# Softmax factors of the first attention on ScalarE, and eight modulation tiles moved behind the attention's row maxima

## The reference

```
mod = silu(c) @ w_mod + b_mod            # 6 chunks of 1024 per layer, for x and for ctx
h   = rms_norm(x) * (1 + scale) + shift  # scale, shift: chunks of mod
qkv = h @ w_qkv                          # 16 query heads, 4 key and value heads, head size 64
q, k = rope(q), rope(k)                  # latent tokens
s   = q @ k.T                            # blocks of 128 queries: up to 3 near key blocks and the 256 context keys
m   = max(max(s), sink)
e   = exp(s - m)
p   = e / (sum(e) + exp(sink - m))
o   = p @ v ;  y = o @ w_o               # y is then gated by another chunk of mod
```

## Time and profile before

| what | value |
|---|---|
| median of the runs | 2658.0 us |
| the profiled execution | 2659.49 us, its span 2656.7 us |
| mean granted TensorE clock over the span | 0.965 of full speed |
| TensorE matmuls busy | 2461.1 us (93%) |
| TensorE weight loads busy | 2036.7 us (77%) |
| VectorE busy | 1693.7 us (64%) |
| ScalarE busy | 1088.6 us (41%) |
| GpSimd busy | 94.3 us (4%) |
| stretch of the attention loop | 205.9 to 405.3 us of the span |

### The profile page before, as it was taken

How to read it: one execution, slowest core, us unless ns; L and a number is a source line. 1 busy time by engine, 2 the same in 40 slices (tenths; PEclk the granted TensorE clock), 3 DMA queues, 4 the chain that set the end, 5 groups by cost and what they waited for, 6 DMA issues and landing times. The chain is left out here.

```text
span 2656.7 us, 32750 instructions
## 1 busy us (share of the span) xinstructions
PE 2461.1 (93%) x12252; PEld 2036.7 (77%) x12252; DVE 1693.7 (64%) x2746; ACT 1088.6 (41%) x1739; POOL 94.3 (4%) x111
## 2 busy tenths in 40 slices
PE   6968899899999999899998899998989999999999
PEld 5865558699999997687777688886766666777777
DVE  6666778765646466655553634445347997569986
ACT  4424443431313133423333422333446663377764
POOL 0000000000000000000000000000000330020000
PEclk8989999899999999889999999998999999999999
DMA  6220004133323232011111122222121221149995
GB/s 255 84 91 0 1 1 159 51 133 127 127 96 127 103 127 82 22 48 48 40 40 48 63 97 96 101 91 94 64 72 44 72 71 64 49 164 341 338 336 183
DMA packets 78131, 275.62 MB, mean 104 GB/s; under 512 B 8800, under 2 KB 9312, under 8 KB 77856
## 3 DMA queue, kind: packets, MB, share of 16 engines
q1 hardware_dynamic: 74016, 265.74, 28.5%
q10 hardware_dynamic: 3968, 7.88, 0.9%
HBM read 271.49 MB, written 2.10 MB: 103 GB/s over the span
## 5 line engine op out<-in xcount | busy, mean ns | idle before, releaser
L645 PE MATMUL DP<-HH,WL 128*128 128x384 f32 (+2 forms) x1408 | 517.7, 368 | 28.3 <-DVE WL L638 22.5
L646 PE MATMUL DP<-HH,WH 128*128 128x384 f32 (+2 forms) x1408 | 504.6, 358 | 0.0
L647 PE MATMUL DP<-HL,WH 128*128 128x384 f32 (+2 forms) x1408 | 504.5, 358 | 0.0
L638 DVE TENSOR_TENSOR WL<-RAW,WH 128x1024 fp32r<-128x1024 f32 x230 | 280.8, 1223 | 218.7 <-ACT WH L611 212.0
L645 PE MATMUL DP<-A,WL 128*128 128x384 f32 (+2 forms) x1072 | 381.7, 356 | 22.6 <-issue 8.4
L646 PE MATMUL DP<-A,WH 128*128 128x384 f32 (+2 forms) x1072 | 379.1, 354 | 0.0
L647 PE MATMUL DP<-A,WH 128*128 128x384 f32 (+2 forms) x1072 | 378.8, 353 | 0.0
L611 ACT ACTIVATE WH<-RAW 128x1024 fp32r<-128x1024 f32 x230 | 241.2, 1050 | 292.6 <-PE DP L647 205.0
L645 PEld LDWEIGHTS DP<-HH,WL 128*128 128x128 f32 x1408 | 267.5, 190 | 66.8 <-DVE WL L638 31.8
L646 PEld LDWEIGHTS DP<-HH,WH 128*128 128x128 f32 x1408 | 267.6, 190 | 29.2 <-issue 5.2
L647 PEld LDWEIGHTS DP<-HL,WH 128*128 128x128 f32 x1408 | 267.3, 190 | 25.5
(11 more groups left out here) (419 smaller groups left out, 3863.7 us busy)
## 6 DMA issues: line engine op xcount, KB each, us to landing
RAW<-in_stream SPq DMA_DIRECT2D x326, 512.0 KB, 3.3
MRAW<-in_stream SPq DMA_DIRECT2D x168, 512.0 KB, 5.4
MATS<-in_ssm ACTq DMA_DIRECT2D x16, 256.0 KB, 2.6
X<-in_x SPq DMA_DIRECT2D x8, 384.0 KB, 10.0
BW<-in_rel ACTq DMA_DIRECT2D x4, 512.0 KB, 3.5
out<-X SPq DMA_DIRECT2D x8, 256.0 KB, 2.0
COND<-in_cond SPq DMA_DIRECT2D x1, 1024.0 KB, 4.9
CONST<-in_const SPq DMA_DIRECT2D x1, 256.0 KB, 4.9
```

Source lines behind the costliest of these rows:

```text
L638: dve.tensor_tensor(WL[:, w, :], RAW[:, nxt.u % RING, :], WH[:, w, :].bitcast(F32), ALU.subtract).then_inc(raw_done[nxt.u % RING], 1)
L645: pe.matmul(out, al, bh, start=first, stop=False)
L646: pe.matmul(out, ah, bh, start=False, stop=False)
L647: return pe.matmul(out, ah, bl, start=False, stop=last)
```

## The change

- `rides_after` gives one modulation tile for r = 2 to 5 and none for r = 6 to 9. The other eight (20 to 27) go into the stream behind the last qkv tile and ahead of the first `attn_w_o` tile, and VectorE takes one at the end of its program for each odd block n below 16 of the attention, behind `maxima(n+2)`.
- `mod_add_bias` for the twelve tiles moves behind the attention loop.
- The denominators' transpose, reciprocal and transpose back leave VectorE. ScalarE makes the factors of block n-1 as exp(-ln(d)) on all 64x512 values, in `denominators(n-1)`: a Ln from PSUM and an Exp in place, put into its program of block n between `sink_term(n+1)` and the second exponentials.
- `normalise` on VectorE waits for that and keeps its two multiplications.

```diff
 def rides_after(t):
-    return (1 if t < 4 else 2) if t < 8 else 0
+    return 1 if t < 4 else 0
+
+def rides_within(n):
+    return 1 if n % 2 and n < 16 else 0
...
     for t in (8, 9, 0, 1, 2, 3, 4, 5, 6, 7, 10, 11):
         dense("attn_w_qkv", t * P)
         for _ in range(rides_after(t)):
+            mod(0, next(rides))
+    for n in range(24):
+        for _ in range(rides_within(n)):
             mod(0, next(rides))
     dense("attn_w_o", 0)
...
+            def denominators(n):
+                act.wait_ge(sem("attended"), values_through(n))
+                if n:
+                    act.wait_ge(sem("normalised"), 2 * n)
+                over = RC[0:64, :, :, :].rearrange("p e j n -> p (e j n)")
+                act.activation(over, XP[64:P, 2 + n % 2, :], ACT.Ln).then_inc(sem("denominators"), 1)
+                act.wait_ge(sem("denominators"), 2 * n + 1)
+                act.activation(over, over, ACT.Exp, scale=-1.0).then_inc(sem("denominators"), 1)
...
                     exps(first + i)
                     if i == 0 and n + 1 < len(WORK):
                         sink_term(n + 1)
+                    if i == 0 and n:
+                        denominators(n - 1)
...
+            denominators(n)
             mixed_high(n, g, b)
...
             rope_low(9)
-            mod_add_bias(dve, 12, lambda n, o=0: slice(o + 16, o + 16 + n))
...
             def normalise(n):
-                dve.wait_ge(sem("attended"), values_through(n))
                 bank_of = 2 + n % 2
-                turned = RCT[:, :].rearrange("p (b n) -> p b n", n=32)
-                dve.transpose(RCT[:, :], XP[64:P, bank_of, :]).then_inc(sem("denominators"), 1)
-                dve.wait_ge(sem("denominators"), 3 * n + 1)
-                dve.reciprocal(RCS[:, :], turned[:, :, 0:1].rearrange("p b n -> p (b n)")).then_inc(sem("denominators"), 1)
-                dve.wait_ge(sem("denominators"), 3 * n + 2)
-                dve.transpose(RC[0:64, :, :, :].rearrange("p e j n -> p (e j n)").rearrange("p (b n) -> p b n", n=32),
-                              RCS[:, :].unsqueeze(2).to_broadcast((64, 16, 32))).then_inc(sem("denominators"), 1)
-                dve.wait_ge(sem("denominators"), 3 * n + 3)
+                dve.wait_ge(sem("denominators"), 2 * n + 2)
...
                 if n + 2 < len(WORK):
                     maxima(*WORK[n + 2][0:4])
+                mods(rides_within(n))
+            mod_add_bias(dve, 12, lambda n, o=0: slice(o + 16, o + 16 + n))
             normalise(n)
```

More of the change, by code:

```diff
@@ L259, in backbone_kernel @@
             RC = sb(s0, "RC", [P, 2, 2, P])
-            RCT = sb(s0, "RCT", [64, 512])
-            RCS = sb(s0, "RCS", [64, 16])
             OU = sb(s0, "OU", [P, 2, 2, P])
```

## The result

| | before | changed |
|---|---|---|
| median of the runs | 2658.7 us (11 runs, 2656.5 to 2666.2) | 2667.3 us (11 runs, 2662.3 to 2672.2) |
| changed against before | | 1.0029, 95% interval 1.0019 to 1.0039 |
| profiled execution, its span | 2659.5, 2656.7 us | 2663.9, 2662.2 us |
| VectorE, ScalarE busy | 1693.7, 1088.6 us | 1653.1, 1119.0 us |

The change made the kernel slower, by about 0.3%. The forecast was 2660, and the range, 2649 to 2669, holds the median. The case with the highest chance (0.55: no difference that a measurement tells from none) was not the one that came.

What follows compares the result with a forecast made beforehand. VectorE was taken to bound the late projection and mostly TensorE the attention; -14.7 us in the projection and +16.6 us in the attention gave +1.9 us on a 2658.0 median, put down as 2660, range 2649 to 2669.

Steps and rivals of the forecast that it cites:

- The projection: Late projection steps: without eight modulation tiles TensorE becomes the bound and value groups start at 160.3 instead of 175.06, -14.7 us.
- the tail: End of the projection: last swap at 152.2, then RoPE, high parts, low parts and split, value groups at 160.3.
- the value groups' clock: Value groups after the projection: starting at full clock would give 2.6 us more; not counted, 0.87 assumed before and after.
- No table reload: Ln and Exp pair in the attention: no activation table loads; the rival with reloads cost +61 us, chance 0.02.
- the attention's term: Attention loop: the pair delays exponentials 1 by 1.17 us and moved tiles delay some blocks, +16.6 us in sum.
- the four-key blocks: Seven attention blocks: key block 3 already waits for exponentials 1, so all 1.17 us reach TensorE, +8.2 us.
- The five-key blocks: Eight attention blocks: key block 3 has 0.2 to 0.5 us of slack, so 0.6 late each, +4.8 us.
- The four two-key blocks: Blocks 5, 11, 17, 20, no tile ahead: ScalarE's chain to `rows_low` replaces VectorE's, 0.1 us each, +0.4 us.
- the rival's 2668: Attention loop: grown stalls make the clock fall, 1.75 us each time; 2665 with three falls, 2677 with ten; chance 0.20.
- The three two-key blocks behind a tile: Blocks 2, 8, 14: a 2.71 us tile replaces 1.77 us on VectorE, +0.95 on `rows_low` each, +2.9 us.
- the other five tiles: Moved tiles ahead of four-key blocks: VectorE ends 3.6 us behind the sink term, `rows_high` 3.9, so covered at no cost.
- The margin within a projection step: Late projection: swap to split done takes 7.2 us, ending 8.3 us into TensorE's 9.2 us step.

Runs made afterwards that it cites:

- e3: The eight tiles moved, factors left on VectorE, and the tiles' sums left out, against the kernel before: 2642.7 us, ratio 0.9931 to 0.9956.
- e9: The change itself run again on another chip, against the kernel before: 2666.5 us, ratio 1.0024 to 1.0048, loop 220.6 us.
- e2: Only the factors moved to ScalarE, all twelve tiles left in the projection, against the kernel before: 2678.1 us, ratio 1.0070 to 1.0100.
- e1: Only the eight tiles moved, factors left on VectorE, against the kernel before: 2670.4 us, ratio 1.0043 to 1.0069.
- e4: The change with ScalarE's pair behind exponentials and queries, VectorE reordered and tiles at other blocks, against the kernel before: 2636.4 us, ratio 0.9910 to 0.9935.

## Why the prediction was right in its range and too low in its sum

**The projection** went as argued: TensorE's step of 9.2 us became the bound (9.18), the tail is that of the forecast (8.13 us from swap to value groups, 8.1 forecast), the value groups start at 159.4 (160.3 forecast), 14.7 us were forecast and 14.0 (e3) to 14.8 (traces) measured. Not counting the value groups' clock was right too: 0.87 before and after, behind a gap of 6.21 us.

**No table reload, loads free, bias additions free**: the last activation table load up to 490 us is still the one asked for by name at the start, as in the earlier trace rows, e3's loop is that of before, and from the last sum to the norm it is 75.3 us in both kernels. The Trainium skill, "ScalarE: Activation LUTs", section "Table sets: the hidden batching unit", would have charged the pair with loads if another set had been active; the trace agrees in that it has no load beside the pair.

**The step that failed is the attention's term**, +16.6 us, where the loop measured +24.2. The mechanism was right: the pair is in a hand-over from ScalarE to TensorE that had no slack, and every four-key block pays its whole length. The size was wrong in two ways.

- The clean cost was 20.9 us, 4.3 over the forecast. I let the chain overlap at each end by 0.1 us, as exponentials 1 did behind the sink term. Here the Ln starts 0.03 after the sink term's end, and exponentials 1 start 0.03 after the Exp's: neither overlaps, so the hand-over is 1.41 and not 1.17. In the four-key blocks, 1.43 for 1.17, that makes 1.8 us over the seven. The five-key blocks have 0.85 for 0.6, 2.1 us over the eight, and that is the same 0.24. In block 9 the fourth key block comes 1.23 us later behind the third than before (280.72 - 278.69 against 285.77 - 284.97), so its slack was 0.17, less than the 0.2 to 0.5 that I gave it. But the fifth no longer waits, and it and what follows give back 0.37: 1.41 - 0.17 - 0.37 = 0.87, which is what that block lost. The two together, 0.54, are close to the 0.57 by which the forecast went from 1.17 to 0.6. The four two-key blocks where I had ScalarE's chain just replace VectorE's cost 1.2 instead of 0.4, 0.26 to 0.47 each. Their third row-wise scores show most of it; block 20, first before and then after:

```profile
384.91 0.39 PE L1188 MATMUL DP<-KDH,A 128*128 128x256 f32 x1 [0.44 <-DVE TOP L2521]
```
```profile
391.57 0.39 PE L1194 MATMUL DP<-KDH,A 128*128 128x256 f32 x1 [0.75 <-DVE TOP L2540]
```

VectorE waits there 0.37 us for `rows_high`, so ScalarE's chain is the longer one, and the first row-wise scores come 2.91 instead of 2.82 us behind the sum: +0.09. Then VectorE waits 0.63 us for `mixed_high`, and its maxima start 0.95 instead of 0.63 us behind those scores: +0.32 where I had put "0.1 or so".

- The clock fell in the loop, as a rival had it: three times in the profiled execution and four in e9, at 1.6 us each but one of 0.2. 24.2 - 20.9 = 3.3 us. I gave it 0.20 and treated it as a case beside the forecast; it is a term on top of it. Its price, 1.75, was a little high; three falls, the count behind its 2665, were right. That the rival's 2668 came so near the measured 2667.3 is luck: the falls made only a seventh of the loop's increase, and the rest of what it had over the forecast came of the stalls. The Trainium skill, "TensorE: Matmul & The Clock Gate", section "HAM oscillation — how this bites in real kernels", has waits that come back in every pass of a loop send TensorE to half clock each time. Those are waits for loads, longer than the stalls here, so it did not follow from it that all ten blocks would pay. The trace agrees with it in part: stalls of up to 1.7 us that come back do send TensorE to its lower level, but three or four times in 24 blocks, at other blocks in e9 than in the first profile.

**A size that was right, and how little the tiles had to do with it.** The three two-key blocks behind a tile cost 2.6 us for 2.9 forecast, and in them the reason holds: TensorE waits 0.96 us for `rows_low` instead of 0.63 and starts the row-wise scores 3.57 us behind block 8's sum instead of 2.83. But e2 has 0.45 of each without any tile, by ScalarE's chain as in block 20, so the tile put only about 0.3 (0.6 in one) on top of it. And the other five tiles were covered, as argued, but only because ScalarE's pair made VectorE wait: without it e1 is 2.16 us longer in three of the five, and has a stall of 3.15 us in block 8.

**In sum**: -14.8 + 20.9 + 3.3 = +9.4, against +8.6 in the medians; the forecast was +1.9. The range held the median by its upper edge, which was there for the clock, while more than half of what the loop had over its forecast (4.3 of 7.6 us) was no clock at all: that it was in range is in part luck. (The margin within a projection step adds up to 7.1 and 8.1 us from the rounded terms, not 7.2 and 8.3; nothing hangs on it.) I had set the limit at which the forecast would be wrong at a loop 22 us longer for "clock, or waits that cost", and it is 24.2 longer for both.

## What to carry to other kernels

Work moved to an idle engine is placed before it is costed: the pair of activations costs 20 us over the loop in the hand-over to TensorE, and delays no key block some 4.5 us later in the same in-order program, behind what TensorE and VectorE wait for. Look for the wait that the receiving engine really has, and put the work behind the last instruction ahead of that wait. When two moves are made together, measure each alone as well: here each hid the other's cost, and the sum of the separate costs (+26.6 and +22.7 in the loop) was twice the cost of both together (+24.2).

## What the runs showed of the hardware beyond what I had expected

- Activations overlap by some 0.1 us or not at all, and the trace doesn't say by what rule. In the change the Ln starts 0.03 behind the sink term and exponentials 1 start 0.03 behind the Exp, though neither needs the other's result; in e4 exponentials 1 start at 269.07, 0.10 before the sink term (268.95 + 0.22) ends, the Ln 0.08 before the activation ahead of it (272.72 + 0.85) ends, and the one behind the Exp 0.10 before it ends. Where a link's overlap is counted, its ends belong in the range: here 0.24 in each hand-over, a sixth of its 1.41.
- The clock fell in the change's loop though TensorE's longest wait for exponentials there is 1.7 us, half of the 3.24 of the earlier trace rows. It fell for some 3.4 us each time and at different blocks in two executions, and a fall cost 1.6 us, or 0.2 where its slower matmuls filled a wait. Filling the stalls with matmuls of no use removed all falls.
- Of the exact condition nothing is settled: other blocks with the same stalls had no fall. Open too is the share of the whole time that the falls are worth, where 2.6 us stand within the intervals.
